# Starting addresses of the TensorE operands in a two-layer hybrid decoder trunk: 64 and 192 unused bytes per partition

## What is computed

```python
def reference(x, mem, positions, norm1, w_out, ..., w_gate_up, w_down, a_w_in, ..., b_w_in, ...):
    for i in range(DEPTH):                                   # DEPTH = 2
        h = rmsnorm(x, norm1[i])
        if i % N_MIXERS == 0:
            mix, xq = mlstm_mixer(h, a_w_in[j], ...)         # p = h @ w_in first
        else:
            mix, xq = diff_attention(h, positions, b_w_in[j], ...)
        xo = memory_cross_attention(xq, mem, mem_norm[i], w_mem_kv[i], ...)
        x = x + jnp.concatenate([mix, xo], axis=-1) @ w_out[i]
        h = rmsnorm(x, norm2[i])
        gu = h @ w_gate_up[i]
        x = x + (jax.nn.silu(gu[..., :FFN_HIDDEN]) * gu[..., FFN_HIDDEN:]) @ w_down[i]
    return x
```

## The kernel before

| tile | role | start | modulo 256 |
|---|---|---|---|
| xT | residual | 1152 | 128 |
| Hh, Hl | moving, 512 columns | 17536, 33920 | 128 |
| Ah, Al | moving, 512 and 256 columns | 50304, 66688 | 128 |
| w_raw | DMA target | 83072 | 128 |
| w_hi, w_lo | stationary | 99456, 113792 | 128 |
| cn | identity and masks | 128128 | 128 |
| tc_hi, tc_lo | moving, 256 columns | 169152, 197824 | 192 |
| wg | stationary, gates of layer 0 | 218112 | 0 |

## Time and profile before

### The profile page before, as it was taken

The page is one execution under the profiler, slowest core; times in us unless marked ns, Lnnn a source line. Parts: engine busy times, 40 slices in busy tenths (PEclk is TensorE's granted clock), DMA queues, the critical chain, the costliest instruction groups (busy, mean ns, idle before and its releaser), DMA issues.

```text
span 1202.2 us, 18736 instructions
## 1 busy us (share of the span) xinstructions
PE 1196.8 (100%) x6998; PEld 1032.9 (86%) x6998; DVE 755.9 (63%) x1099; ACT 502.4 (42%) x1012; POOL 857.4 (71%) x873
## 2 busy tenths in 40 slices
PE   9999999999999999999999999999999999999998
PEld 7888887788889998899888777778888899889997
DVE  7954434645737991599335888874674599348931
ACT  7522456733203551355231666644431255125510
POOL 7998433566878996699676444445688799669965
PEclk9999999999999999999999999999999999999999
DMA  7234211132223333233433222232232333322332
GB/s 282 92 123 157 71 36 53 53 106 79 92 83 106 106 106 123 88 106 106 126 103 97 80 71 71 64 80 69 71 100 79 118 106 107 105 89 98 115 105 85
DMA packets 35097, 117.43 MB, mean 98 GB/s; under 512 B 4417, under 2 KB 4930, under 8 KB 34886
## 3 DMA queue, kind: packets, MB, share of 16 engines
q1 hardware_dynamic: 33416, 112.83, 29.2%
q10 hardware_dynamic: 1598, 3.51, 1.2%
HBM read 111.07 MB, written 2.11 MB: 94 GB/s over the span
## 4 chain that ended last, share of the span: by engine, by line
PE 97%; DVE 1%; ACT 1%; issue 0%; ACTq 0%; POOL 0%; POOLq 0%
PE PS L1946 69%; PE PS L2284 26%; PE PS L2385 1%; DVE Al L1564 0%; PE PS L2194 0%; PE PS L2413 0%; PE PS L2354 0%; DVE nmB L1850 0%; PE PS L2019 0%; PE PS L2346 0%; PE PS L2338 0%; DVE PB L1862 0%; ACT tmp L1010 0%; ACT tmp L1018 0%; DVE PB L1861 0%
## 5 line engine op out<-in xcount | busy, mean ns | idle before, releaser
L783 POOL TENSOR_TENSOR w_lo<-w_raw,w_hi 128x256 fp32r<-128x256 f32 (+1 forms) x516 | 394.7, 796 | 11.0
L778 POOL TENSOR_SCALAR w_hi<-w_raw 128x1024 fp32r<-128x1024 f32 (+2 forms) x132 | 142.1, 1076 | 283.4 <-PE PS L1946 275.0
L2284 PE MATMUL PS<-tc_hi,w_hi 128*128 128x256 f32 x896 | 250.9, 280 | 0.0
L2284 PE MATMUL PS<-tc_hi,w_lo 128*128 128x256 f32 x896 | 250.0, 279 | 0.0
L2284 PE MATMUL PS<-tc_lo,w_hi 128*128 128x256 f32 x896 | 250.0, 279 | 0.0
L1946 PE MATMUL PS<-Hh,w_hi 128*128 128x512 f32 x560 | 229.3, 410 | 0.0
L1946 PE MATMUL PS<-Hl,w_hi 128*128 128x512 f32 x560 | 219.1, 391 | 0.0
L1946 PE MATMUL PS<-Hh,w_lo 128*128 128x512 f32 x560 | 219.0, 391 | 0.0
L1946 PE MATMUL PS<-Ah,w_hi 128*128 128x512 f32 (+1 forms) x544 | 208.0, 382 | 0.1
L1946 PE MATMUL PS<-Ah,w_lo 128*128 128x512 f32 (+1 forms) x544 | 205.0, 377 | 0.0
L1946 PE MATMUL PS<-Al,w_hi 128*128 128x512 f32 (+1 forms) x544 | 204.9, 377 | 0.0
(11 more groups left out here) (300 smaller groups left out, 1805.5 us busy)
## 6 DMA issues: line engine op xcount, KB each, us to landing
w_raw<-in_wt_dram SPq DMA_DIRECT2D x181, 512.0 KB, 3.6
w_raw<-in_wt_dram SPq DMA_DIRECT2D x16, 384.0 KB, 3.0
w_raw<-in_wt_dram SPq DMA_DIRECT2D x8, 448.0 KB, 3.3
QKR<-QKP ACTq DMA_DIRECT2D x24, 128.0 KB, 4.8
xT<-in_x_t_dram SPq DMA_DIRECT2D x8, 256.0 KB, 4.8
out_dram<-xT SPq DMA_DIRECT2D x8, 256.0 KB, 2.0
mT<-in_mem_t_dram SPq DMA_DIRECT2D x1, 1024.0 KB, 9.5
cn<-in_constants_dram SPq DMA_DIRECT2D x1, 594.5 KB, 6.9
```

What stands on the lines that cost most here:

```text
L778: nc.gpsimd.tensor_scalar(w_hi[:, sl, 0:nk], w_raw[:, raw, 0:nk], 0.0, 1.0, ALU.add, ALU.mult).then_inc(w_round, 1)
L783: lo = nc.gpsimd.tensor_tensor(w_lo[:, sl, w], w_raw[:, raw, w], w_hi[:, sl, w].bitcast(F32), ALU.subtract)
L2284: last = nc.tensor.matmul(out_, w[:, b + k], a[:, q, k], start=q < 4 and k == 0 and j == 0, stop=k == 3 and j == 2, skip_group_check=q > 3)
```

## The change

Two tiles that nobody reads or writes are allocated: 64 bytes a partition ahead of `xT`, 192 bytes ahead of `w_hi`. No instruction is added, taken away or moved on any engine; the lists of instructions of the two kernels are the same but for line numbers. Only addresses differ. `xT`, `Hh`, `Hl`, `Ah`, `Al` and `w_raw` lie 64 bytes further on, and so at 192 modulo 256. `w_hi` and all that follows, `tc_hi`, `tc_lo`, `cn` and `wg` among them, lie 64 + 192 = 256 bytes further on, and keep their remainder modulo 256 (modulo 512 it changes for all of these: the split weights go from 128 to 384, `tc_hi` and `tc_lo` from 192 to 448).

```diff
         PS = ctx.enter_context(nc.psum_tensor("PS", [P, 8, 512], F32))
 
 
+        sb("shift_x", [P, 16])
         xT = sb("xT", [P, KD, SEQ])
         Hh = sb("Hh", [P, KD, SEQ], F32R)
         Hl = sb("Hl", [P, KD, SEQ], F32R)
         Ah = sb("Ah", [P, 8, SEQ], F32R)
         Al = sb("Al", [P, 8, SEQ], F32R)
         w_raw = sb("w_raw", [P, RAW, 8, P])
+        sb("shift_w", [P, 48])
         wq_hi = sb("w_hi", [P, 28, P], F32R)
         wq_lo = sb("w_lo", [P, 28, P], F32R)
```

## The result

The changed kernel is slower: median 1206.96 us of 7 runs (1205.04 to 1207.69), against 1202.78 us of 7 runs of the kernel before (1202.60 to 1204.62). The ratio is 1.0032, with an interval of 1.0020 to 1.0043. The forecast was 1195.6 us, a gain. The time lies inside the range of 1189 to 1214 us, but on the other side of no change: rival 2 came true, at a price smaller than it was given. That the range held it is no merit of the sum; the range reached to both sides of no change.

A forecast was written before the change was run, and what follows sets the result against it. PE was taken as the bound, cost being one matmul's pitch times their number. Gains of 0.4 us (memory projection) and 6.9 us (dense matmuls), zero elsewhere, made 7.3 us off 1202.9: 1195.6 us, range 1189 to 1214 us.

The forecast's parts named there:

- rival 2: The dense 512-column stream settles on a worse pitch, 3 to 6 ns more: 1211.9 to 1221.2 us; chance 0.24.
- (a): The 192 memory projection matmuls of 256 columns go from 120.0 to 117.8 ns, the pairs' pitch: 0.4 us gained.
- (b): The 3120 dense matmuls of 512 columns each get 2.2 ns cheaper, from 226.7 to 224.5 ns: 6.9 us gained.
- (c): The 2688 pair matmuls keep remainders modulo 256: zero; with a period of 512 or more, 5.9 us lost or similar gain.
- (d): ScalarE, VectorE, GpSimd and DMAs use tiles 64 bytes further on: zero, any slowdown covered by waits for PE.
- Rival 1: Addresses don't matter and nothing moves; 120.0 against 117.8 ns has another cause: 1202.9 us; chance 0.15.
- Rival 3: The address period is over 256 bytes, so the pairs lose up to 5.9 us: up to 1208.8 us; chance 0.05.
- rival 4: The dense 512-column surcharge comes down to half, 6.7 ns off, 20.9 us gained: 1182 us; chance 0.10.

The follow-up runs named there:

- the table: Separate kernel of 72-matmul streams, computing nothing of the trunk, with chosen operand starts: pitches by distance, 226.7 to 234.2 ns (512 columns), 116.7 to 120.0 (256).
- e1: Changed kernel without the 192 bytes ahead of the weights, so both operands move by 64 and all distances stay: 1202.81 us against 1202.83, ratio 0.9999.
- e5: Against the changed kernel: nothing ahead of `xT`, 64 bytes ahead of the weights; dense matmuls at distance 192, pairs still at 64: 1218.39 us, ratio 1.0129.
- e2: Against the changed kernel: nothing ahead of `xT`, 256 bytes ahead of the weights, so all remainders modulo 256 are the old ones: 1203.13 us, ratio 1.0004.
- v3: Kernel before the change with only the pairs' moving operands moved, to byte 240, distance 112 from the split weights: 1198.82 us, ratio 0.9967.
- m2: Separate stream kernel with finer distances, other widths and fewer stationary columns: 512 columns at distance 0 took 230.0 ns with 64 stationary columns, 231.6 with 32.
- v1: Against the changed kernel: both shifts removed, only the pairs' moving operands moved, to byte 160, distance 32 from the split weights: 1199.70 us, ratio 0.9974.

## Why the prediction was wrong

**What bounds the kernel** was right: PE alone, and the cost of one matmul times their number. The long dense pieces of every run are pitch times count, and so are the stages of pairs in which PE doesn't wait.

**(a), the memory projection,** was right: 120.0 to 118.2 as read from the rows, 117.8 in the table. 0.4 us.

**(b) is the step that failed.** It carried a difference of 2.2 ns, seen at 256 columns, over to 512 columns, because the surcharge at byte 128 was 13.4 ns for one width and 13.3 for the other. The table shows that this equality was chance: at distance 64 the surcharges are 15.6 ns (512 columns) and 11.1 (256), at 32 they are 20.0 and 10.0. The two widths have their own curves over the distance, and at distance 0 one is at its lowest and the other at its highest. The 2.2 ns came out with the other sign, 226.7 to 228.9, and 3120 x 2.2 = 6.9 us lost would be the twin of the forecast gain. Not all of it is: 2083 matmuls in the long pieces lose 4.31 us, but the other 1037, in the stretches broken by small matmuls, lose only about 1 us (0.27 in the attention stretch, 0.29 + 0.4 at the start), 0.9 ns each. The prediction had taken the full 2.2 ns for them too, for want of a row. The prediction had named this as what would make it wrong, and gave it a chance of 0.24. A clue lay in its own material: 226.7 was nearly the lowest of the pitches that the stream went through, which speaks for a place from which one can hardly gain.

The prediction also described the cause as where the moving operand starts. In its rows every stationary operand of a steady stream lay at 128, so start and distance could not be told apart; e1 and e5 do that.

**(c), the pairs,** was right in that the period is 256 (e2), and wrong in the zero: in the profiled execution they gained 2.25 us. The reason is neither of those that it weighed. The dense stream ahead of them has another rhythm, and a stage that is entered behind its longest step runs at 113.3 ns for a while. It was not on the list, since the trace of before has no stage in that state.

**(d), the other engines,** was right. The longest waits of the changed kernel:

```profile
POOL w_hi L780 <- PE PS L1948: 272.6, 97, 9.9
```

GpSimd still waits for PE for 272.6 us, against 275.0 before. The prediction said that a PE that got a few us faster would still find the others ready. That holds over the whole kernel and is wrong in the pairs: there GpSimd has 0.1 us to spare in 9.90, and v3 shows the bound.

**The rivals.** Rival 1, that addresses don't matter, falls by e5 (1.3% for 64 bytes) as well as by the result. The Trainium skill, "TensorE: Matmul & The Clock Gate", section "Back-to-back issue gap", gives spacings that follow from the columns alone: N / 2.4 GHz and 2.5 ns for a matmul by itself, about 216 ns for 512 columns, and about 131 ns in a stream with a weight load for each matmul. For the fp32r streams here neither holds: the runs show 226.7 to 238.2 ns for 512 columns by distance alone. "SBUF — State Buffer", section "Who interferes with whom", calls PE's two read ports independent. That doesn't fit a pitch that depends on the distance between the starts of the two operands. Its sentence "PE and ACT never wait on anyone" is about other engines, and no run here tests it. Rival 2 was right, with 2.2 ns where it had 3 to 6, and so 1206.96 us instead of 1211.9 to 1221.2. Its argument, that most other pitches lie above 226.7, is what the table shows. Rival 3 falls by e2; rival 4 falls by the result, and no distance tried comes below 226.7.

**What stays open** is the mechanism. The distance modulo 256 between the starts of the two operands sets the pitch, together with the entry, and that two reads get in each other's way is a guess. That the surcharge is the length of the weight load is refuted by m2, and why one width prefers 0, another 32 or 112, and a third none isn't explained by any run.

## What to carry to other kernels

Where PE is the bound, measure the pitch of the kernel's own matmul forms in a small stream kernel, over the distance between moving and stationary start modulo 256, each width by itself, and behind the stream that really precedes it; then place the tiles by that table, as v1 did. A difference seen at one width is no forecast for another, and a pitch that is already the lowest of those in the trace is a reason not to touch the addresses. Before counting on a shorter pitch, compare the length of a stage's step with the pace of the engines that make its operands and free its banks.

## What the runs showed of the hardware

- The pitch of an fp32r matmul depends on the distance modulo 256 bytes between the starts of its moving and its stationary operand: 226.7 to 238.2 ns for 512 columns, 113.3 to 120.0 ns for 256, nothing for 384 at the three distances tried (173.3 ns).
- At one and the same address a stream of 256 columns has two steady pitches, 113.3 and 117.8 ns (distance 64), or 113.3 and 118.7 (distance 16). Which one it takes goes with how it is entered: at distance 64, behind 512 columns at distance 64, 113.3 after a last step of 231 or 232 ns and 117.8 after 226 to 230; at distance 16, 113.3 behind small matmuls and 118.7 behind 512 columns at distance 0. A wait of PE can end the shorter pitch, and doesn't always.
- A steady stream can step unevenly with period 3 (226, 229, 232 ns), so a pitch has to be read over a multiple of three steps.
- Fewer stationary columns don't make it cheaper at distance 0: 226.7 ns with 128, 230.0 with 64, 231.6 with 32. At distance 32, 64 columns take 230.9 ns against 233.3.
